# A two-stage front end (modulation, then first norm) made into one stage, with four modulation pieces formed later by GpSimd

## The chip, the cores and the metric

The kernel runs on one core of one Trainium2 chip. The metric is the device time of one execution in microseconds (us), as the median of several runs. A core has a matrix engine (TensorE, PE in the profile, its weight loads PEld), a vector engine (VectorE, DVE), an activation engine (ScalarE, ACT), a general engine (GpSimd, POOL) and an engine that here only starts transfers (SyncE, SP). Engines work through their own instruction streams in order and wait for each other by semaphores. SBUF is the on-chip memory of 128 partitions, PSUM the smaller one that the matrix engine writes.

## The reference

One layer of a diffusion backbone with 2048 latent tokens and 256 context tokens of width 1024. Only the start of it matters here:

```python
sc_lat = jax.nn.silu(c)                 # (1, 1024)
sc_ctx = jax.nn.silu(c_ctx)             # (1024,)
m_lat = split(sc_lat @ w_mod + b_mod, 6)      # w_mod is (1024, 6 * 1024), 24 MB
m_ctx = split(sc_ctx @ w_mod + b_mod, 6)
h_lat = rms_norm(x_lat, norm1_g) * (1 + m_lat[1]) + m_lat[0]
h_ctx = rms_norm(x_ctx, norm1_g) * (1 + m_ctx[1]) + m_ctx[0]
p = h @ w_in                            # the projection, 1024 x 4640
...                                     # two head groups, output projection
x = x + m_lat[2] * y                    # gate; m_lat[3], m_lat[4] modulate the second norm,
                                        # m_lat[5] is the gate of the MLP
```

Pieces 0 and 1 (shift and scale) are needed for the latents and for the context before the projection can start. Pieces 2 to 5 are needed for the latents only, and only in the last stage, after the scans.

## The kernel before

The program is a row of stages (`phase_mod`, `phase_norm`, `phase_project`, `phase_gdn`, `phase_hgrn`, `phase_merge`, `phase_out`). Each stage is a block in which every engine has its own stream. A stage starts on an engine when all engines have ended the one before. Inside a stage the order on each engine is the order in which the code is written, and semaphores tie the engines to each other.

`phase_mod` (L99 to L233). SP loads a few small vectors, then `w_mod` in six pieces of 4 MB into `wm`, two buffers. DVE multiplies each of a piece's eight slices `k` (128 input rows by 1024 columns) by a per-partition number of `sc` and adds it up in `acc` (L214, L217). For pieces 0 and 1 it does so twice, once for the latents and once for the context (`accx`). PE then sums `acc` over the partitions with products of one column (L161, L166), and DVE adds the bias and forms `e.gain` (L227 to L232).

`phase_norm` (L239 to L352). There are five blocks of tokens, one of 256 (context), and four of 512 in a hardware loop. For a block SP loads the tokens (L274), PE transposes them into `pt` (L286), ACT copies them to `xt` (L308) and stores them (L311). DVE squares `xt` slice by slice (L331), PE sums the squares with a matrix of ones (L293), ACT takes the root (L315), DVE the reciprocal of the whole 128x512 result (L333). Then for each slice `k` there are three operations on DVE, the product with the reciprocal (L348), scale and shift (L340) and the remainder `h_lo` (L343), and one on ACT, the rounded half `h_hi` (L319). `h_hi` and `h_lo` are the two halves in which the projection reads its input.

`phase_project` (L364 to L796). For each of 36 tiles of 128 output columns (and a small tile of 32, called ab, at the start), ACT and DVE split the weights into `whi` and `wlo` (L577, L702). PE forms each tile in five groups of tokens (four where the context isn't wanted), each of 24 products into `pg`, with 512 tokens a product (L527). For the first 12 tiles (q, k, v) ACT and DVE do a short convolution and for the first eight a normalisation (L603 to L623, L736 to L751), whose sums run on PE (L541). Tiles are grouped in kinds of four (`KINDS`, L357). GpSimd has nothing to do in these three stages.

```python
331     dve.tensor_tensor(sq[:, k % 2, 0:n], xt[:, k, 0:n], xt[:, k, 0:n], ALU.mult)
333     dve.reciprocal(rt[:, 0:n], rt[:, 0:n])
348     dve.tensor_tensor(ht[:, k % 2, 0:n], xt[:, k, 0:n], rt[:, 0:n], ALU.mult)
455     sp.dma_start(raw[:, 0, :, 0:AB_W], win[:, :, AB_COL:AB_COL + AB_W])
531     pe.wait_ge(w_lo, 1)
```

## Time and profile before

| what | us |
|---|---|
| median of 3 runs | 4352.18 |
| lowest and highest | 4346.83, 4361.99 |
| the profiled execution's own time | 4353.56 |
| its span in the trace | 4351.8 |
| PE busy, share of the span | 83% |
| DVE, ACT, POOL busy | 43%, 32%, 16% |

The profiled execution's time is 1.8 us above its span. The trace holds one execution; times in it are counted from the span's start. A row of the timeline is start, duration, engine, line, operation and operands, and in brackets how long the engine had been idle and what released it. "SPq" and "ACTq" are the issues of transfers. In the views that group instructions, a group's mean duration is in nanoseconds. A product of two plain float32 matrices is two instructions on PE, each with its own weight load; a transpose or a product of the rounded kind (float32r) is one.

### The profile page before, as it was taken

How to read it: one execution, taken by the hardware profiler on the slowest of the kernel's cores; microseconds unless marked ns; L12 is line 12 of the kernel's file. 1: busy time of each engine (PE TensorE's matmuls, PEld its weight loads, DVE VectorE, ACT ScalarE, POOL GpSimd, SP SyncE). 2: the span in 40 equal slices, each digit the busy share in tenths (PEclk: the TensorE clock that was granted, in tenths of full speed). 3: DMA queues.
4: the chain of work that ended last, by engine and by line, in shares of the span. 5: the costliest groups of instructions: out<-in, count | busy, mean ns of one | idle time of the engine just before them, and what ended most of it. 6: DMA issues, size and time to landing. Idle time of an engine off the chain costs nothing. (4 is left out here: it accounts for less than half of the span.)

```text
span 4351.8 us, 98698 instructions
## 1 busy us (share of the span) xinstructions
PE 3614.9 (83%) x42292; PEld 2976.9 (68%) x42292; DVE 1880.8 (43%) x2660; ACT 1377.6 (32%) x1858; POOL 697.0 (16%) x752
## 2 busy tenths in 40 slices
PE   2549999999968888857674428899999888999998
PEld 2327788888857777747664227688888666888886
DVE  7647851111025555545546943523323335233233
ACT  0336641433125555513332212312212223122122
POOL 0000000000035555505556102000000220000002
PEclk9779999999979999966777668899999888999998
DMA  6412232243223333354442263111111231111111
GB/s 234 145 43 49 54 80 75 99 130 100 72 95 109 108 106 113 104 105 85 102 86 70 68 217 107 35 48 52 44 52 46 81 107 35 49 52 44 52 46 58
DMA packets 460370, 365.08 MB, mean 84 GB/s; under 512 B 115908, under 2 KB 413192, under 8 KB 454408
## 3 DMA queue, kind: packets, MB, share of 16 engines
q1 hardware_dynamic: 430088, 315.94, 25.2%
q0 software_dynamic: 6912, 25.17, 1.7%
q10 hardware_dynamic: 23168, 20.97, 1.6%
q8 instruction: 164, 2.69, 0.3%
q14 instruction: 38, 0.31, 0.0%
HBM read 262.64 MB, written 99.39 MB: 83 GB/s over the span
## 5 line engine op out<-in xcount | busy, mean ns | idle before, releaser
L2289 PE MATMUL o_pg<-o_h_hi,o_w_hi 128*128 128x512 f32 x1280 | 516.9, 404 | 70.6 <-DVE o_h_lo L2438 48.6
L527 PE MATMUL p_pg<-h_hi,p_whi 128*128 128x512 f32 (+3 forms) x1384 | 531.4, 384 | 25.5 <-DVE p_wlo L702 25.5
L527 PE MATMUL p_pg<-h_lo,p_whi 128*128 128x512 f32 (+3 forms) x1384 | 519.3, 375 | 0.0
L527 PE MATMUL p_pg<-h_hi,p_wlo 128*128 128x512 f32 (+3 forms) x1384 | 519.3, 375 | 0.0
L2290 PE MATMUL o_pg<-o_h_lo,o_w_hi 128*128 128x512 f32 x1280 | 509.1, 398 | 0.0
L2291 PE MATMUL o_pg<-o_h_hi,o_w_lo 128*128 128x512 f32 x1280 | 509.0, 398 | 0.0
L2289 PE MATMUL o_pg<-o_f_hi,o_w_hi 128*128 128x512 f32 x1024 | 398.3, 389 | 0.0
L2290 PE MATMUL o_pg<-o_f_lo,o_w_hi 128*128 128x512 f32 x1024 | 398.3, 389 | 0.0
L2291 PE MATMUL o_pg<-o_f_hi,o_w_lo 128*128 128x512 f32 x1024 | 398.3, 389 | 0.0
L2289 PEld LDWEIGHTS o_pg<-o_h_hi,o_w_hi 128*128 128x128 f32 x1280 | 245.6, 192 | 150.8 <-issue 46.9
L527 PEld LDWEIGHTS p_pg<-h_hi,p_whi 128*128 128x128 f32 (+1 forms) x1384 | 258.4, 187 | 81.5 <-DVE p_wlo L702 26.3
L2360 ACT ACTIVATE o_w_hi<-o_raw 128x1024 fp32r<-128x1024 f32 x144 | 151.4, 1052 | 484.1 <-PE o_pg L2291 464.7
L2491 DVE SCALAR_TENSOR_TENSOR o_x<-o_pg,mod,o_x 128x512 f32<-128x512 f32 x128 | 96.1, 751 | 469.6 <-PE o_pg L2291 469.6
L527 PEld LDWEIGHTS p_pg<-h_lo,p_whi 128*128 128x128 f32 (+1 forms) x1384 | 258.3, 187 | 55.0 <-issue 6.0
L527 PEld LDWEIGHTS p_pg<-h_hi,p_wlo 128*128 128x128 f32 (+1 forms) x1384 | 258.1, 186 | 50.1
L2291 PEld LDWEIGHTS o_pg<-o_h_hi,o_w_lo 128*128 128x128 f32 x1280 | 247.0, 193 | 52.6
L2290 PEld LDWEIGHTS o_pg<-o_h_lo,o_w_hi 128*128 128x128 f32 x1280 | 247.5, 193 | 48.4
L2482 DVE TENSOR_TENSOR o_tmp<-o_tmp 128x512 f32<-128x512 f32 x128 | 88.6, 692 | 438.1 <-ACT o_f_hi L2409 438.1
L2427 DVE TENSOR_TENSOR o_w_lo<-o_raw,o_w_hi 128x1024 fp32r<-128x1024 f32 x144 | 195.9, 1361 | 71.3 <-ACT o_w_hi L2360 71.3
L2406 ACT ACTIVATE o_tmp<-o_pg 128x512 f32<-128x512 f32 x128 | 76.5, 598 | 470.0 <-PE o_pg L2291 470.0
L2291 PEld LDWEIGHTS o_pg<-o_f_hi,o_w_lo 128*128 128x128 f32 x1024 | 192.3, 188 | 39.9
L2289 PEld LDWEIGHTS o_pg<-o_f_hi,o_w_hi 128*128 128x128 f32 x1024 | 192.3, 188 | 39.9
(279 smaller groups left out, 6265.6 us busy)
## 6 DMA issues: line engine op xcount, KB each, us to landing
o_raw<-in_w_mlp SPq DMA_DIRECT2D x128, 512.0 KB, 4.1
g_kqvb<-scr_kqv SPq DMA_DIRECT2D x72, 384.0 KB, 3.5
mod_w<-in_w_mod SPq DMA_DIRECT2D x6, 4096.0 KB, 13.1
p_raw<-in_w_in SPq DMA_DIRECT2D x38, 512.0 KB, 5.9
g_kqa<-scr_kqv SPq DMA_DIRECT2D x72, 256.0 KB, 3.0
scr_kqv<-p_y SPq DMA_DIRECT2D x24, 576.0 KB, 4.9
scr_hf<-p_y SPq DMA_DIRECT2D x16, 576.0 KB, 5.3
scr_hk<-p_s SPq DMA_DIRECT2D x16, 576.0 KB, 8.2
```

Of the source, the lines that this page charges most:

```text
L527: last = nc.tensor.matmul(pg[0:m, bank, 0:n], w[:, q, k, 0:m], h[:, k, hoff:hoff + n], start=(k == 0 and j == 0), stop=(k == KT - 1 and j ...
L2289: nc.tensor.matmul(out, w_hi[:, p, k, :], half(rhs[0], k, h), start=(k == 0), stop=False)
L2290: nc.tensor.matmul(out, w_hi[:, p, k, :], half(rhs[1], k, h), start=False, stop=False)
L2291: last = nc.tensor.matmul(out, w_lo[:, p, k, :], half(rhs[0], k, h), start=False, stop=(k == KT - 1))
L2360: nc.scalar.activation(w_hi[:, p], raw[:, p], ACT.Copy).then_inc(w_hi_ready, 1)
L2406: nc.scalar.activation(tmp[:, (2 * s + h) % 4, :], pg[:, 2 * (s % 2) + h, :], ACT.Relu).then_inc(rectified, 1)
L2427: dve.tensor_tensor(w_lo[:, p], raw[:, p], w_hi[:, p].bitcast(F32), ALU.subtract).then_inc(w_lo_ready, 1)
L2482: dve.tensor_tensor(slot, slot, slot, ALU.mult).then_inc(f_sq, 1)
L2491: dve.scalar_tensor_tensor(half(x1, m, h), pg[:, 2 * (s % 2) + h, :], e.mod[:, M_GATE2 + m:M_GATE2 + m + 1], half(x1, m, h), ALU.mult, ALU ...
```

## The change

`phase_mod` and `phase_norm` become one stage, `phase_front`. What it does:

- Only pieces 0 and 1 of `w_mod` are loaded there, 8 MB in eight slices of 1 MB (rows `k`, 2048 columns), into four buffers that lie in the space of `h_lo`. PE multiplies each slice with the two columns of `sc` (latents, context) as the stationary side, 4 products of 512 columns a slice (`products`), and adds up in PSUM. ACT and DVE copy the two rows out (`mrow`), PE turns them into columns with 16 transposes, DVE adds the bias and forms the gain.
- Tokens are loaded in tiles of 128 rows. ACT (three tiles of a block, and both of the context) and DVE (one tile) square each row and add it up in the same instruction (`square`). The root and the reciprocal are taken of 128x4 numbers. DVE puts them on a diagonal (`diag`), and PE spreads them over all partitions with four products with the ones (`spread`).
- Per slice `k`, ACT copies the transposed tokens (`copy`) and forms `h_hi` (`high`). DVE forms product, gain and norm in one operation (`scale`) and the remainder in another (`low`). The squares of the next block stand among the slices of the present one.
- The 14 small loads move from SP to ACT. The tokens' transpose is stored by SP in two halves a block. The first two weight loads of the projection are issued in the front stage.
- `h_hi` and `h_lo` are five tensors each, one for each block.
- In `phase_project` GpSimd forms pieces 2 to 5 in eight sums `c` of 512 columns. For each of a sum's eight slices it loads 256 KB from its own queue, multiplies by `sc` and adds to `macc`. After every fourth tile PE sums `macc` over the partitions (`mod_sums`, 4 products of one column) into unused columns of bank 0 of `pg`. At the end of the stage DVE adds the bias and forms the second gain.

The core of the diff:

```diff
+                for k in range(4):
+                    load_w(k)
+                load_x(0)
+                for k in range(4, KT):
+                    load_w(k)
+                load_x(1)
+                load_x(2)
...
+                store(1)
+                load_x(3)
+                store(2)
+                load_x(4)
+                store(3)
+                store(4)
...
+                def products(k):
+                    pe.wait_ge(wm_in[k % 4], 16 * (k // 4 + 1))
+                    for n in range(4):
+                        last = nc.tensor.matmul(mp[0:2, n, :], e.sc[:, k, :], wm[k % 4][:, n, :],
+                                                start=(k == 0), stop=(k == KT - 1))
...
+                def spread(b):
+                    pe.wait_ge(diag_ready, b + 1)
+                    if b >= 2:
+                        pe.wait_ge(u_ready, 8 * (b - 1))
+                    for a in range(BLOCKS[b][0]):
+                        last = nc.tensor.matmul(mp[:, b % 2, a * P:(a + 1) * P], e.ones, diag[:, a, :], start=True, stop=True)
...
+                for b in range(1 + NB):
+                    for k in range(KT + 1):
+                        if k < KT:
+                            copy(b, k)
+                        if k >= 1:
+                            high(b, k - 1)
+                        if 1 <= b < NB and 3 <= k < 6:
+                            square(b + 1, k - 3)
+                        if 1 <= b < NB and k == 6:
+                            roots(b + 1)
...
+                    dve.scalar_tensor_tensor(ur[:, g % UR, 0:n], xt[:, g % RING, 0:n], e.gain[:, g0 + k:g0 + k + 1],
+                                             mp[:, b % 2, 0:n], ALU.mult, ALU.mult).then_inc(u_ready, 1)
...
+                    dve.scalar_tensor_tensor(e.h_lo[b][:, k, :], ur[:, g % UR, 0:n], e.mod[:, s0 + k:s0 + k + 1],
+                                             e.h_hi[b][:, k, :].bitcast(F32), ALU.add, ALU.subtract).then_inc(lo_ready, 1)
...
+                def mod_sums(c, released):
+                    pe.wait_ge(m_acc, c + 1)
+                    pe.wait_ge(group_free, released)
+                    for s in range(TB // P):
+                        last = nc.tensor.matmul(modps[:, c * 4 + s:c * 4 + s + 1], macc[:, s * P:(s + 1) * P],
+                                                e.ones[:, 0:1], start=True, stop=True)
...
+                    pool.wait_ge(mw_in[x % 2], 16 * (x // 2 + 1))
...
+                        nc.gpsimd.tensor_scalar(w, w, sc, None, ALU.mult).then_inc(m_part, 1)
+                        pool.wait_ge(m_part, done + 1)
+                        nc.gpsimd.tensor_tensor(macc[:, :], macc[:, :], w, ALU.add).then_inc(m_part, 1)
+                        done += 2
...
+                    if x + 2 < MC * KT:
+                        load(x + 2)
```

How the instructions stand, first on DVE at the end of the modulation (before), where `mod_acc` is the running sum of a piece:

```order
L214 TENSOR_SCALAR mod_acc<-mod_w,mod_sc 128x1024
L217 SCALAR_TENSOR_TENSOR mod_acc<-mod_w,mod_sc,mod_acc 128x1024 x7
L227 TENSOR_TENSOR mod<-mod_ps,cols 128x48
L228 TENSOR_TENSOR mod<-mod_ps,cols 128x16
L232 SCALAR_TENSOR_TENSOR gain<-mod,cols 128x8 x3
```

and on PE in the changed front stage, where `n_wm_50` to `n_wm_53` are the four buffers of `w_mod`, `n_pt` the transposed tokens, `n_mrow` the two modulation rows and `n_diag` the diagonals:

```order
L211 MATMUL n_mp<-n_wm_52,sc 2x512 x4
L211 MATMUL n_mp<-n_wm_53,sc 2x512 x4
L222 MATMUL n_pt<-cst,n_x 128x128 x6
L248 MATMUL n_cc<-cst,n_mrow 128x2 x16
L231 MATMUL n_mp<-n_diag,cst 128x128 x2
L222 MATMUL n_pt<-cst,n_x 128x128 x10
L222 MATMUL n_pt<-cst,n_xb 128x128 x4
L231 MATMUL n_mp<-n_diag,cst 128x128 x4
L222 MATMUL n_pt<-cst,n_xb 128x128 x28
```

The weighted sum over the input rows has moved from DVE to PE, which does it 4 products at a time as the slices come in. One block's first transposes stand ahead of the `spread` for it, the other 28 behind it.

DVE in a block of 512 tokens, before (from the squares to the second slice):

```order
L331 TENSOR_TENSOR n_sq<-n_xt 128x512
L332 REGISTER_ALU
L333 RECIPROCAL n_rt<-n_rt 128x512
L348 TENSOR_TENSOR n_ht<-n_xt,n_rt 128x512 x2
L340 TENSOR_SCALAR n_ht<-n_ht,gain,mod 128x512
L343 ISA
L343 TENSOR_TENSOR h_lo<-n_ht,h_hi 128x512
L348 TENSOR_TENSOR n_ht<-n_xt,n_rt 128x512
```

and now (the end of one block and the start of the next; `n_u` is what `scale` writes):

```order
L394 SCALAR_TENSOR_TENSOR n_u<-n_xt,gain,n_mp 128x512
L402 SCALAR_TENSOR_TENSOR h_lo<-n_u,mod,h_hi 128x512
L375 RECIPROCAL n_rs<-n_rs 128x4
L380 TENSOR_SCALAR n_diag<-cst,n_rs 128x128 x4
L402 SCALAR_TENSOR_TENSOR h_lo<-n_u,mod,h_hi 128x512
L394 SCALAR_TENSOR_TENSOR n_u<-n_xt,gain,n_mp 128x512 x2
```

Three operations for a slice are two, the eight squares are one instruction elsewhere in the block, and the reciprocal is of 4 columns in place of 512, followed by four products for the diagonal.

PE in the projection, at the end of the fourth tile (now; `p_macc` is GpSimd's sum):

```order
L608 MATMUL p_pg<-h_hi,p_wlo 128x512
L622 MATMUL p_pn<-p_s,cst 128x512
L628 MATMUL p_pg<-cst,p_macc 128x1 x4
L608 MATMUL p_pg<-h_hi,p_whi 128x256
L608 MATMUL p_pg<-h_lo,p_whi 128x256
```

The row of four one-column products is new, and stands at eight such places; before, a tile's last product was followed at once by the next tile's first.

## Rows read from the trace of the kernel before

**Rows 1.** Busy time of each engine by stage (granted clock, share of the DMA engines, GB/s)

```profile
0.00:109.00 109.00, 28.91 (x130) 28.11 (x130) 78.70 (x80) 3.05 (x5) 0.21 (x4) 1.00 0.61 234
109.00:263.00 154.00, 66.72 (x224) 41.56 (x224) 108.52 (x166) 55.15 (x87) 0.00 (x0) 0.72 0.34 120
263.00:340.00 77.00, 51.84 (x226) 34.16 (x227) 26.00 (x20) 27.11 (x31) 0.00 (x0) 0.79 0.11 25
340.00:590.00 250.00, 235.94 (x1057) 184.97 (x1056) 204.46 (x167) 164.04 (x214) 0.00 (x0) 1.00 0.26 59
590.00:1222.00 632.00, 631.00 (x2952) 529.31 (x2951) 87.99 (x100) 193.31 (x228) 0.00 (x0) 1.00 0.32 93
```

**Rows 2.** Timeline, from the start to the first norm's first block

```profile
0.75 1.28 ACT L174 ACT_TABLE_LOAD   x1 [0.75 <-PEq L2552]
...
1.20 0.42 SPq L135 DMA_DIRECT2D mod_rows<-in_b_mod  x1
...
6.98 74.30 SPq L149 DMA_DIRECT2D mod_w<-in_w_mod  x6
...
104.34 3.57 PE L161 MATMUL mod_ps<-cst,mod_acc 128*128 128x1 f32 x16 [8.81 <-DVE mod_acc L217]
...
113.75 3.63 PE L286 MATMUL n_pt<-cst,n_x 128*128 128x128 f32 x16 [5.84 <-DMA n_x<-in_ctx]
```

**Rows 3.** Timeline, roots of two blocks running, then the norm's end and the projection's start

```profile
207.13 0.69 ACT L315 ACTIVATE n_rt<-n_pq,eps 128x512 f32<-128x512 f32 x1 [7.06 <-PE n_pq L293]
...
237.86 0.69 ACT L315 ACTIVATE n_rt<-n_pq,eps 128x512 f32<-128x512 f32 x1 [7.06 <-PE n_pq L293]
...
257.84 0.69 DVE L343 TENSOR_TENSOR h_lo<-n_ht,h_hi 128x512 f32 x1 [0.15 <-DVE n_ht L340]
...
263.34 0.42 PE L527 MATMUL p_pg<-h_hi,p_whi 128*32 128x256 f32 x1 [25.52 <-DVE p_wlo L702]
```

**Rows 4.** Timeline of PE, the last four float32 instructions of 512 columns in a block

```profile
143.56 1.99 PE L293 MATMUL n_pq<-n_sq,cst 128*128 128x512 f32 x4
```

**Rows 5.** Groups of ACT between 108 and 264 us (busy, mean ns | idle before)

```profile
L319 ACT ACTIVATE h_hi<-n_ht,mod,gain 128x512 f32 x32 | 25.6, 812 | 47.7 <-DVE n_ht L348 47.7
L308 ACT ACTIVATE n_xt<-n_pt 128x512 f32<-128x512 f32 x32 | 17.3, 595 | 2.0 <-PE n_pt L286 1.2
L319 ACT ACTIVATE h_hi<-n_ht,mod,gain 128x256 fp32r<-128x256 f32 x8 | 4.7, 598 | 6.4 <-DVE n_ht L348 6.4
L308 ACT ACTIVATE n_xt<-n_pt 128x256 f32<-128x256 f32 x8 | 3.1, 384 | 104.0 <-PE n_pt L286 103.8
L577 ACT ACTIVATE p_whi<-p_raw 128x1024 fp32r<-128x1024 f32 x1 | 1.1, 1057 | 1.1 <-DMA p_raw<-in_w_in 1.1
```

**Rows 6.** Groups of DVE in the projection: from PSUM, and with two SBUF inputs

```profile
L702 DVE TENSOR_TENSOR p_wlo<-p_raw,p_whi 128x1024 fp32r<-128x1024 f32 x37 | 45.2, 1223 | 245.1 <-ACT p_whi L577 241.3 <-DVE p_s L786 2.9 <-DVE p_s L792 1.0
L741 DVE SCALAR_TENSOR_TENSOR p_y<-p_pg,cols,p_y 128x512 f32<-128x512 f32 x36 | 27.0, 751 | 63.4 <-ACT p_y L603 62.8
L751 DVE TENSOR_TENSOR p_y<-p_y,p_rt 128x512 f32<-128x512 f32 x32 | 22.1, 692 | 1.1
```

**Rows 7.** DMA issues (KB each, median us from issue to landing)

```profile
n_x<-in_ctx SPq DMA_DIRECT2D x1, 1024.0 KB, 4.9
scr_ga<-p_y SPq DMA_DIRECT2D x4, 1024.0 KB, 4.7
```

**Rows 8.** Groups of POOL in the whole span

```profile
L2253 POOL TENSOR_TENSOR o_rt<-o_rt,o_tmp 128x512 f32<-128x512 f32 x56 | 71.7, 1289 | 148.2 <-ACT o_tmp L2367 148.0
L2269 POOL DMA_DIRECT2D o_ring<-scr_xT x16 | 8.8, 548 | 110.4 <-DVE o_x L2447 99.4 <-DVE o_h_lo L2438 11.0
L2250 POOL COPY o_rt<-o_tmp 128x512 f32<-128x512 f32 x8 | 4.8, 615 | 1292.3 <-ACT o_tmp L2367 1292.2
```

**Rows 9.** A DVE group beside a busy POOL, 1226 to 1890 us: two SBUF inputs

```profile
L1342 DVE TENSOR_TENSOR g_z<-g_z,g_vt 128x512 f32<-128x512 f32 x36 | 38.0, 1055 | 0.0
```

**Rows 10.** PE's waits between 340 and 590 us (total us, times, longest)

```profile
PE p_pn L541 <- ACT p_s L614: 14.1, 15, 1.8
```

More of the change, by code:

```diff
@@ new lines, in high @@
+                def high(b, k):
+                    g = 8 * b + k
+                    nt, g0, s0 = BLOCKS[b]
+                    act.wait_ge(u_ready, g + 1)
+                    nc.scalar.activation(e.h_hi[b][:, k, :], ur[:, g % UR, 0:nt * P], ACT.Identity,
+                                         bias=e.mod[:, s0 + k:s0 + k + 1]).then_inc(hi_ready, 1)
+                for a in range(2):
+                    square(0, a)
+                roots(0)
+                for a in range(3):
+                    square(1, a)
@@ new lines, in _ @@
+                roots(1)
+                act.wait_ge(wm_used, KT)
+                nc.scalar.activation(mrow[:, 0:2, :], mp[0:2, 0:2, :], ACT.Copy).then_inc(mrow_act, 1)
+                for b in range(1 + NB):
[8 more added lines that the diff above has]
+                            roots(b + 1)
@@ new lines, in _ @@
+                last.then_inc(mod_ready, 1)
+                dve.wait_ge(mod_ready, 1)
+                for b in range(1 + NB):
+                    for k in range(KT + 1):
+                        if k < KT:
+                            scale(b, k)
+                        if k >= 1:
+                            low(b, k - 1)
+                        if b == 0 and k == 2:
+                            inverse(1)
+                        if 1 <= b < NB and k == 4:
+                            square(b + 1)
+                        if 1 <= b < NB and k == 7:
+                            inverse(b + 1)
```

441 lines of the change are left out of this document (244 added, 197 removed).

## The prediction

> **What bounds the kernel now.** First the busy times by stage [rows 1]. The reader should see two kinds of stage. Up to 263 us PE is busy for 28.9 of 109 and 66.7 of 154 us, and DVE for 78.7 and 108.5: nothing of the projection runs, and everything waits for a chain that goes through DVE. From 590 us on PE is busy for 631 of 632 us; between, from 340, for 235.9 of 250. So a microsecond taken out of the first 263 is a microsecond of the end, and one added to PE after 340 is one too. Second, the timeline of the start [rows 2]: the six loads of `w_mod` are issued until 81 us, the last sums of PE end at 107.9, and the first tokens are transposed at 113.8, because their load is only issued after the stage has ended. Third, the norm [rows 3]: two roots of neighbouring blocks are 30.7 us apart (237.86 - 207.13), the last `h_lo` ends at 258.5, and the first product of the projection starts at 263.3, after a load and a split of its weights. The front end is thus 263.3 us long, 108 of modulation, 6 of waiting for tokens, 145 of norm, 5 to get going.
>
> **The new front stage, step by step.** I add it up to the projection's first product.
>
> 1. Products begin. They need the first slice and the two silu columns. The first slice is SP's fourth issue, at about 2.2 us, and 1 MB lands 4.9 us after its issue [rows 7]: 7.1. ACT first issues 14 small loads; on SP 16 issues took 6.98 - 1.20 = 5.8 us, 0.36 each [rows 2], so 5.1 from 0.75 on, then a table load of 1.28 and the silu: 7.4. Both come together; I take 7.4.
> 2. 32 products of 512 float32 columns, two instructions each. Four such instructions took 1.99 us with the drain of the last [rows 4], so 0.50 at most and 0.46 by my estimate without the drain: 32 x 0.92 = 29.5. The first slice will run at the lower clock, at twice that: +3.7. The loads are not behind: 8 MB and the context's 1 MB, against 234 GB/s as the mean of a stage that was held up by DVE [rows 1], would be 40 us at that rate, and 1 MB in 4.9 us with its latency is already about the pace of 3.7 us a slice with four buffers. End of products: 40.6.
> 3. Two copies out of PSUM of 1024 columns, side by side on ACT and DVE, 2 x 0.6 = 1.2 (0.595 for 512 [rows 5]). 16 transposes: 16 instructions of this size took 3.57 and 3.63 us [rows 2]: 3.6. Bias and gain 0.7. Together 5.5: 46.1. Squares, roots and the first diagonals are done by then, beside the products.
> 4. Context block, paced by ACT: 8 x (0.384 + 0.598) = 7.9 [rows 5]: 54.0.
> 5. A block of 512. ACT: 8 x (0.595 + 0.812) = 11.3, three squares of 1024 columns at 1.06 (the nearest row of that size) = 3.2, root 0.2: 14.7 [rows 5]. DVE: 8 x (0.75 + 0.70) = 11.6 [rows 6], the fourth square 1.3, reciprocal and four diagonals 1.0: 13.9. They run side by side, so 14.7. At the border they don't: the diagonals are made late in DVE's order, PE then needs 8 instructions at 0.22 [rows 2] = 1.8 to spread them, and the first `scale` 0.75 before ACT has a `high`: 2.6. A block is 17.3 in place of 30.7. Three of them: 51.9, and the last, without squares, 11.3 + 0.7. End at 117.9.
> 6. The stage also waits for its last store. It is issued when the last slice is copied, some 2.3 us before the end, and 1 MB takes 4.7 to land [rows 7]: +2.4, 120.3.
> 7. The projection's first weights are there already, so only the two splits of 32 columns and the start of a stage remain: 1.4, where it was 4.8. First product at about **122 us**, 141 earlier.
>
> **Bounds of that.** At best ACT never waits at the borders (-8) and the transposes go at the higher clock (-2): 112. At worst all products run at the lower clock: below.
>
> **What the projection pays.** PE's one-column products move into a stage where PE is full. They are 8 x 4, two instructions each, 64 in all. In the modulation 16 took 3.57 us [rows 2], 0.22 each, 14.3 as the upper bound; the lower is none of it where PE waits anyway. It waits 14.1 us between 340 and 590 [rows 10], where three of the eight places are; five are where it doesn't wait at all. I take 10, since at the higher clock they should be quicker than in that row: range 5 to 14. Waiting for GpSimd is not to be feared: a slice costs it a multiplication, an addition and an issue. Addition 1.29, issue 0.55 [rows 8]; the multiplication isn't in the trace, and lies between the copy, 0.62, and the addition, 1.29. That is 2.5 to 3.1, and with a wait for the load at most 4, so 32 us for a sum; a kind takes PE four tiles, some 90 us (1222 - 340 over 35 tiles is 25 each). The order on GpSimd has nothing else queued. DVE pays at its side: operations with two SBUF inputs take 0.69 for 512 columns in the projection [rows 6], and 1.06 where GpSimd is busy beside it [rows 9], 0.36 more. GpSimd will be busy for a third of each kind. In the q and k kinds DVE is busy for 204 of 250 us [rows 1] and PE's sums hang on it; some 13 such operations meet GpSimd there, 4.7 us on DVE, of which I put 2 on PE (0 to 5). After 590 DVE is idle for most of the time and hides it. The bias and gain at the stage's end are DVE's, while PE still works on its last tile; the 16.8 MB of loads lie where the DMA engines are a quarter to a third busy [rows 1].
>
> The Trainium skill (SBUF — State Buffer, "SBUF: two separate sides") says that DVE and GpSimd share a pair of SBUF ports as an exclusive lock held for a whole instruction, so that a DVE operation with two SBUF inputs is blocked until a GpSimd one ends. The 1.06 against 0.69 agrees in kind, though it is less than a whole GpSimd addition of 1.29; by the rule at its hardest each meeting would cost 1.29 in place of 0.36, so 17 us on DVE in q and k instead of 4.7, and the sum would be worse by up to 12 us. The same page warns that loads issued by GpSimd can be starved by DVE; no row here shows that.
>
> **The sum.** The profiled execution took 4353.6 us: -141 + 10 + 2 = -129, so 4224.6. The median of the runs lies 1.4 below the profiled one: **4223 us**.
>
> **Rivals.**
>
> - *The clock stays low in the products.* They have a stationary side of only two columns, and the trace has no such instruction. For it: in the first 109 us the profile records 1.00, yet 16 instructions took the same 3.6 us as in the stage that was granted 0.72 [rows 1, 2], so the low level, 1.2 GHz, is what such thin work got. Against it: PE has no gaps here. Price: 59 us in place of 33.2, 26 more: 4249. Chance 0.12.
> - *The blocks wait for tokens.* The load of block 3 is issued after block 1 has been copied, behind 1 MB of store. 3 MB then land within some 11 us, and ACT wants the third tile about 10 us into the block. A slower store costs up to 4 us a block, three times: 4235. Chance 0.09.
> - *The projection pays more.* All 37 + 32 operations with two SBUF inputs [rows 6] slowed by 0.36, and PE waiting for each, is 25 us; with 14 of sums: 4250. Against it: after 590 nothing of DVE is urgent. Chance 0.10.
> - *The front is shorter still* (borders hidden, products at the pace of the loads): 4200. Chance 0.06.
> - *Slower than before: PE waits for GpSimd.* `mod_sums` stands in PE's order, and all later tiles are queued behind it. From 263 to the last place, about 1135, there are 872 us for 64 slices. Above 13.6 us a slice PE begins to wait, and above 13.6 + 129/64 = 15.6 the change is slower than before: at 16 it would be 4380. The rows give at most 4, so this needs a load that takes over four times its normal time. Chance 0.03.
>
> **The numbers.** The forecast has 0.60, with 4207 to 4240 as its own range. The range for 8 in 10 takes in the slow tokens, the clock and most of a costlier projection: 4204 to 4258. A measurement of this kernel can tell about 0.3%, 13 us, from no change. All cases but the last are far beyond that: faster 0.96, same 0.01, slower 0.03 (the last case, from a slice of 15.4 us on).
>
> **What would show it.** The first product of the projection at 112 to 130 us; the 32 products in 30 to 36 us at a granted clock of 1.00 (if near 60, the clock rival); neighbouring roots 16 to 19 us apart; before the first `scale`, no wait of PE or ACT for tokens; from there to the projection's end 5 to 20 us more than the 959 of before, with one-column products of 0.1 to 0.22 us each; no wait of PE for `p_macc`; DVE's two-input operations longer in the first third of each kind. After the projection all stages should be as long as before; if one isn't, the sum is wrong in a place that I haven't looked at.

## The result and the profile after

The changed kernel takes 4208.24 us (median of 4 runs, 4195.76 to 4209.89), against 4355.73 us for the kernel before on the same chip (4 runs, 4346.83 to 4361.99). The ratio is 0.9657, 95% interval 0.963 to 0.9683: 3.4% faster. Forecast was 4223 with a range of 4204 to 4258.

| stage | before, us | changed, us | difference | forecast |
|---|---|---|---|---|
| up to the projection's first product | 263.34 | 111.44 | -151.9 | -141 |
| projection, to GpSimd's first MEMSET behind it | 962.95 | 971.05 | +8.1 | +12 |
| all behind | 3125.5 | 3125.3 | -0.2 | 0 |
| span | 4351.8 | 4207.8 | -144.0 | -129 |

The changed kernel by stretch of time, as [rows 1] for before. A row is the stretch, its length, each engine's busy time with its instructions, the granted clock, the share of the DMA engines and GB/s:

```profile
core 0: us, PE busy (x) PEld busy (x) DVE busy (x) ACT busy (x) POOL busy (x), PEclk, DMA share, GB/s
0.00:7.95 7.95, 0.28 (x1) 0.18 (x1) 0.09 (x2) 1.50 (x3) 0.21 (x4) 1.00 0.70 251
7.95:38.40 30.45, 30.45 (x66) 5.67 (x66) 3.33 (x14) 9.17 (x16) 0.00 (x0) 1.00 0.83 322
38.40:41.80 3.40, 2.81 (x31) 2.58 (x30) 1.71 (x5) 1.54 (x3) 0.00 (x0) 1.00 0.02 5
41.80:49.75 7.95, 5.39 (x25) 4.12 (x23) 7.53 (x21) 6.06 (x15) 0.00 (x0) 0.62 0.44 136
49.75:97.80 48.05, 23.23 (x122) 20.00 (x121) 39.50 (x71) 37.01 (x69) 0.00 (x0) 0.68 0.71 254
97.80:111.44 13.64, 3.80 (x26) 2.85 (x24) 10.86 (x17) 9.93 (x17) 0.41 (x1) 0.75 0.40 154
111.44:1082.49 971.05, 927.17 (x4296) 756.77 (x4296) 329.61 (x288) 383.31 (x472) 223.60 (x184) 0.98 0.37 96
1082.49:4207.80 3125.31, 2614.25 (x37706) 2167.75 (x37706) 1376.08 (x2128) 934.80 (x1294) 696.41 (x748) 0.89 0.26 78
```

Read the second row first: PE is busy for all of its 30.45 us, where before the modulation was DVE's and took 109 us [rows 1]. The norm's context block, three full blocks and the last one took 145 us before; they now lie in rows four to six and take 67 us (41.8 to 109.05). The same stretches in the timeline (start, duration, engine, line, operands, number; in brackets the idle time ahead and what ended it), which answer to [rows 2] and [rows 3]:

```profile
6.42 1.28 ACT L279 ACT_TABLE_LOAD   x1 [6.42 <-issue]
7.71 0.18 ACT L279 ACTIVATE sc<-n_cc 128x16 f32<-128x16 f32 x1
7.95 2.72 PE L211 MATMUL n_mp<-n_wm,sc 128*2 128x512 f32 x3 [3.69 <-ACT sc L279]
...
17.68 20.76 PE L211 MATMUL n_mp<-n_wm,sc 128*2 128x512 f32 x48
...
39.84 1.12 PE L248 MATMUL n_cc<-cst,n_mrow 2*128 2x2 f32 x16 [0.59 <-DVE n_mrow L408]
...
59.87 0.29 ACT L300 ACTIVATE n_rs<-n_ss,eps 128x4 f32<-128x4 f32 x1
63.18 2.08 PE L231 MATMUL n_mp<-n_diag,cst 128*128 128x128 f32 x8 [4.86 <-DVE n_diag L380]
65.35 0.75 DVE L394 SCALAR_TENSOR_TENSOR n_u<-n_xt,gain,n_mp 128x512 f32<-128x512 f32 x1 [1.56 <-issue]
66.15 0.60 ACT L310 ACTIVATE n_xt<-n_pt 128x512 f32<-128x512 f32 x1 [3.44 <-PE n_pt L222]
75.90 0.29 ACT L300 ACTIVATE n_rs<-n_ss,eps 128x4 f32<-128x4 f32 x1
```

The last 48 product instructions took 20.76 us, 0.43 each. The first ones were slower: three took 2.72 us, with starts 0.85 us apart, twice the 0.43, and the first sixteen took 9.54 us:

```profile
7.95 9.54 PE L211 MATMUL n_mp<-n_wm,sc 128*2 128x512 f32 x16 [3.69 <-ACT sc L279]
```

At 0.43 us each sixteen would take about 7.0, so some six of them ran at the lower level of the clock, 1.2 GHz, behind an idle time of PE of 3.69 us. The table's 1.00 doesn't contradict that: in this trace the records of the granted clock begin at 13.04 us, and a stretch without a record is printed as 1.00.

Two roots are 16.0 us apart (75.90 - 59.87), 30.7 before. At the border between two blocks PE stands 4.86 us for the diagonals and ACT 3.44 us for the transposes queued behind them; e7 returns to that.

In the projection, the two kinds of GpSimd arithmetic and the one-column sums of PE (engine, operation, number: shortest, median, longest in ns, first and last start):

```profile
L669 POOL DMA_DIRECT2D p_mw<-in_w_mod x64: 557/590/1562, 111.0 to 916.7; - x64
L685 POOL TENSOR_SCALAR p_mw<-p_mw,sc x56: 1558/1572/2400, 117.2 to 922.8; 128x512 f32<-128x512 f32 x56
L687 POOL TENSOR_TENSOR p_macc<-p_macc,p_mw x56: 1270/1290/2302, 118.9 to 924.5; 128x512 f32<-128x512 f32 x56
...
  PE p_pg L628: 547.9, 7
```

GpSimd waited for PE for 547.9 us in seven waits (78 us each), and PE never for GpSimd. The whole list of PE's waits in the projection is these two rows (waiting line, released by: us in total, times, longest); the second is the projection's start:

```profile
PE p_pn L622 <- ACT p_s L738: 38.5, 15, 25.0
PE p_pg L608 <- DVE p_wlo L826: 8.6, 1, 8.6
```

### The profile page after: what moved, and what is told of

It is laid out like the page before. It is cut to its first block and busy times, and to the rows that moved or that the text cites. A ratio compares the mean times of both kernels' runs of the same rounds, so it can differ in the third digit from the quotient of the medians.

```text
span 4207.8 us, 98568 instructions
## 1 busy us (share of the span) xinstructions
PE 3607.4 (86%) x42264; PEld 2959.9 (70%) x42264; DVE 1768.7 (42%) x2544; ACT 1383.3 (33%) x1887; POOL 920.6 (22%) x936
```

## The experiments

Eleven variants and a repetition of the changed kernel ran. A single total can't settle a few microseconds here: the stages behind the projection, which no variant touches, took between 3112.7 us (e1) and 3125.5 us (before). The totals were also measured on several chips, on which the median of the kernel before lay between 4352.5 and 4357.4. So the variants are compared by two stretches of their traces, the start of the projection and its length, and where these differ by 3 us or less, by the rows in which they differ. The start itself moves by 1.3 us between kernels with the same front (110.15 to 111.44), mostly because three to seven of the first product instructions run at the lower clock, a different number in each execution. The third column leaves that out: it counts from the end of the products to the projection's first product, and is 72.87 to 73.00 us in all six profiles with an unaltered front.

| kernel | projection starts | from the products' end | its length | total, us (runs) |
|---|---|---|---|---|
| before | 263.34 | - | 962.95 | 4355.73 (4) |
| changed | 111.44 | 73.00 | 971.05 | 4208.24 (4) |
| changed, again | 110.15 | 72.89 | 968.72 | 4201.56 (5) |
| e1, deferral alone | 219.93 | - | 970.03 | 4303.59 (4) |
| e2, four times the sums | 111.27 | 72.98 | 1005.09 | 4236.06 (1) |
| e3, GpSimd only loads | 110.27 | 72.87 | 967.53 | 4201.61 (1) |
| e4, slow GpSimd | 110.46 | 72.87 | 1215.61 | 4447.68 (1) |
| e5, wide reciprocals | 124.27 | 85.75 | 971.26 | 4214.23 (1) |
| e6, tokens behind the modulation | 124.65 | 87.28 | 971.94 | 4215.64 (1) |
| e7, early inverse | 105.26 | 67.41 | 973.61 | 4208.53 (4) |
| e8, GpSimd late | 111.42 | 72.99 | 969.94 | 4207.02 (1) |
| e9, e7 and e8 | 104.85 | 67.11 | 972.56 | 4194.44 (5) |
| e10, DVE's low half twice | 125.07 | 86.91 | 968.85 | 4212.58 (1) |
| e11, ACT's high half twice | 125.90 | 87.23 | 969.20 | 4214.83 (1) |

### e1: the deferral alone

The edit is to the kernel before: two pieces in the modulation stage, and the changed kernel's GpSimd block and shifted sums in the projection.

```diff
-        PIECES = 6
+        PIECES = 2
...
+                def mod_sums(c, released):
...
+            @block.gpsimd
+            def _(pool):
```

> The kernel before with one part of the change alone: the modulation makes two of its six pieces ahead of the projection, and GpSimd forms the other four while the projection runs, with the sums over partitions between the projection's tiles. The first modulation stage and the first norm stay two stages in the old form. My theory: the four pieces left out were about 12 us each of the stage that waits for the loads and for GpSimd, so the time ahead of the projection falls by about 50 us (263 to about 213 us), the projection grows by 8 us as in the changed kernel (eight places of 1.0 us), the later stages stay: total about -42 us, near 4312. The rival: most of the gain is the deferral, since the modulation stage is bound by the eighteen pieces of work on six pieces, and the stage falls to a third (109 us to about 37): time ahead of the projection -73 us, total -65, near 4289. A third: the projection pays more without the merged front, because DVE and GpSimd compete as they did there: projection +20 or more.

Measured: ratio to before 0.9887 (0.9871 to 0.9904), -49 us. By stage (the old norm is the second row):

```profile
0.00:65.30 65.30, 14.62 (x66) 14.16 (x66) 39.36 (x45) 3.05 (x5) 0.21 (x4) 1.00 0.34 133
65.30:219.93 154.63, 66.78 (x225) 41.49 (x225) 108.97 (x168) 55.21 (x87) 1.25 (x2) 0.73 0.34 119
219.93:1189.96 970.03, 926.32 (x4296) 756.03 (x4296) 327.61 (x288) 383.89 (x472) 225.54 (x182) 0.98 0.37 96
```

The start of the projection moves by 43.4 us, not by 50 or 73: each piece left out gives 43.4 / 4 = 10.9 us. The old stage goes on at 65.3 where it went on at 109; the norm is unchanged (154.6, before 154.3). The projection pays 7.1 us. So the first theory (213 us and a projection 8 us longer) is nearer than its two rivals, a start 73 us earlier and a projection 20 us longer. The deferral alone is worth 36 us by the stages that it touches, a quarter of the change's 144; the other 13 us of its total lie in stages that it doesn't touch. The larger part of the change is the merged stage: 219.93 - 111.44 = 108.5 us, of which the modulation by PE's products is 65.3 - 41.8 = 23.5 and the norm the remaining 85.

### e5, e6: two parts of the norm undone

```diff
-                    dve.reciprocal(rs[:, t:t + n], rs[:, t:t + n]).then_inc(inv, 1)
...
                         dve.wait_ge(bc_ready, b + 1)
+                        dve.reciprocal(mp[:, b % 2, 0:n], mp[:, b % 2, 0:n]).then_inc(inv, 1)
```

> The changed kernel with one part of the new norm undone: the reciprocal of the root is taken of the row spread over 128x512 (3.35 us each, 1.75 us for the context's 256 columns, as in the kernel before) in place of the 128x4 column ahead of the spreading. My theory, that a block's period of 16.0 us ends on VectorE around the border between blocks, since ScalarE is busy for 12.35 us of it: the reciprocal stands after the spreading and ahead of the block's first product, so each of the blocks pays its 3.35 us in full, 4 x 3.35 + 1.75 = 15 us later start of the projection (111.4 to about 126.5). The rival, that ScalarE's copies and roundings bound the block: the reciprocal lies beside them and the start moves by under 5 us.

Measured: the projection starts 12.8 us later. The reciprocals by themselves (first of a block, then the next):

```profile
70.01 3.37 DVE L388 RECIPROCAL n_mp<-n_mp 128x512 f32<-128x512 f32 x1 [1.57 <-PE n_mp L231]
88.69 3.37 DVE L388 RECIPROCAL n_mp<-n_mp 128x512 f32<-128x512 f32 x1 [1.58 <-PE n_mp L231]
```

The period is 18.68 us against 16.02: 2.66 of the 3.37 are paid; the rest is hidden, presumably beside what the other two engines had left to do meanwhile. The first theory holds, somewhat weaker than its 15 us.

In e6 the loads of the tokens go behind the modulation, and the first block's squares with them:

```diff
-                for k in range(4):
+                for k in range(KT):
                     load_w(k)
+                sp.wait_ge(mod_ready, 1)
                 load_x(0)
-                for k in range(4, KT):
-                    load_w(k)
                 load_x(1)
```

> The changed kernel with another part undone: the tokens' loads wait until the modulation is done, as they did in the kernel before, and the squares and sums of the first block move behind them into the context block. The theory of the merged stage: ahead of the context block stand now a load's landing (4.9 us), the transposes, copies and squares of it (3 to 5 us) and the first root and reciprocal (about 3 us), and the context block itself gets the first token block's squares on top: the start of the projection moves from 111.4 to about 124 us (12 to 14 us later). The rival: what stands ahead of the blocks is hidden under the 30 us of the modulation's products anyway, so little of the 152 us gained comes from the overlap: under 5 us later.

Measured: 13.2 us later, 14.3 counted from the end of the products, as the first theory had it:

```profile
40.21 0.25 DVE L408 SCALAR_TENSOR_TENSOR gain<-mod,cols 128x8 f32<-128x8 f32 x2
44.16 1.06 ACT L291 ACTIVATE n_junk<-n_x 128x1024 f32<-128x1024 f32 x1 [5.74 <-DMA n_x<-in_ctx]
...
46.58 1.28 ACT L299 ACT_TABLE_LOAD   x1
47.87 0.29 ACT L299 ACTIVATE n_rs<-n_ss,eps 128x2 f32<-128x2 f32 x1
...
50.35 0.87 DVE L388 SCALAR_TENSOR_TENSOR n_u<-n_xt,gain,n_mp 128x256 f32<-128x256 f32 x2 [1.40 <-PE n_mp L230]
```

Gain and bias are there at 40.5, and the first scaling comes at 50.35 in place of 41.82: load, squares, table, root, diagonals and spreading stand in a row, 8.5 us. The other 4.7 lie behind it, where the context block now has the token squares of the first block as well. e5 and e6 account for 27 of the norm's 85 us, if their costs may be added. The rest, 58 us, wasn't undone piece by piece, so its cause is argued and not shown: three DVE operations on a slice became two, and the squares left DVE and PE, three tiles of four for ACT. What the traces show is DVE's busy time between modulation and projection, 108.8 us before, 57.9 now (7.53 + 39.50 + 10.86), and the same in one period from root to root, before and now:

```profile
207.13:237.86 30.73, 14.49 (x48) 8.80 (x48) 23.44 (x33) 11.30 (x17) 0.00 (x0) 0.72 0.36 139
59.87:75.90 16.03, 7.46 (x40) 6.51 (x40) 13.04 (x24) 12.34 (x25) 0.00 (x0) 0.71 0.71 262
```

Of the 14.7 us that a period lost, DVE's busy time lost 10.4 and its idle time 4.3.

### e10, e11: which engine paces a block

```diff
+                    if b < NB:
+                        dve.scalar_tensor_tensor(e.h_lo[NB][:, k, 0:n], ...)
```

e10 repeats DVE's second operation of a slice, e11 in the same way the rounding on ACT.

> The changed kernel with VectorE's second operation on every slice of the norm (the low half) issued twice in all blocks but the last, the extra one into memory that the last block overwrites; same result. It adds 8 x 0.66 = 5.3 us of VectorE's time to each block of 512 tokens; VectorE is busy for 13.0 and ScalarE for 12.3 of a block's 16.0 us. Theory A, the prediction's: ScalarE's 14.7 us pace a block and VectorE's work lies beside it with some 3 us to spare, so the period grows by 5.3 - 3.0 = 2.3 us, to about 18.3. Theory B: VectorE sets the pace, since the chain at the border between two blocks (reciprocal, diagonals, first product) is its own, so it pays all of it: period 21.3 us, start of the projection 3 x 5.3 + 2.6 = 18 us later (about 129 us in place of 111.4; by theory A about 119).

> The counterpart: ScalarE's rounding to the high half issued twice on every slice in all blocks but the last; same result. It adds 8 x 0.5 to 0.6 = 4 to 4.9 us of ScalarE's time to a block. Theory A, ScalarE paces a block: it pays all of it, period 20 to 20.9 us, start of the projection about 3 x 4.5 + 2 = 15 us later (near 127 us). Theory B, VectorE sets the pace and ScalarE has 16.0 - 12.3 = 3.7 us to spare: the period grows by about 1 us, to 17.2, and the start by 4 us, to 115. Should both kernels pay in full, a block is one chain that goes through both engines, and neither paces it alone.

Measured: period 19.77 us with DVE's operation doubled (roots at 63.64 and 83.40) and 20.15 us with ACT's (65.54 and 85.69). ACT pays nearly in full: added activations start 0.61 us apart though each lasts 0.72, so eight of them are 4.9 us, of which the period pays 4.13. DVE pays 3.74 of 5.3 us. The projection starts 13.9 us later with DVE's work doubled, between theory A's 7.6 and theory B's 17.6, and 14.2 us later with ACT's, as theory A said (15). So theory A is right on ACT and too generous on DVE, which has 1.6 us to spare in a block, not the 3.0 of its idle time. Neither engine paces a block alone: work added to either is mostly paid, ACT's a little more than DVE's. In e11 DVE waits 5.2 us for ACT's copies, and ACT for nothing ahead of the added operation (groups, busy, mean ns | idle before and what ended it, 65 to 105 us):

```profile
L397 DVE SCALAR_TENSOR_TENSOR n_u<-n_xt,gain,n_mp 128x512 f32<-128x512 f32 x17 | 12.7, 746 | 8.3 <-ACT n_xt L310 5.2 <-issue 3.1
L317 ACT ACTIVATE h_lo<-n_u,mod 128x512 fp32r<-128x512 f32 x17 | 12.3, 723 | 0.0
```

### e2, e3, e8: what the projection pays for

e2 makes each place's four one-column products sixteen; e3 leaves pieces 2 to 5 of the modulation out of the computation (GpSimd loads the weights but only fills its sum with a constant); e8 computes all, but behind the projection's first twelve tiles, with a place after every second tile there.

```diff
-                    for s in range(TB // P):
+                    for s in [t % 4 for t in range(4 * TB // P)]:
```

> The changed kernel with the four one-column products in each of the eight places between the tiles made sixteen (each column written four times, same result). It tells apart what makes the projection of the changed kernel 8.1 us longer than before (971.05 against 962.95 us). Theory A, the shifted sums themselves: 1.0 us per place of four products, so twelve more cost 3.0 us a place and the projection grows by about 24 us, to about 995 (up to 37 us if each added product costs its two weight loads of 192 ns in full). Theory B, contention of DVE with GpSimd: TensorE waits for DVE's longer operations, and the added products change little, under 5 us.

```diff
-                        nc.gpsimd.tensor_scalar(macc[:, :], w, sc, None, ALU.mult).then_inc(m_part, 1)
+                        nc.gpsimd.memset(macc[:, :], 0.5).then_inc(m_part, 1)
...
-                        nc.gpsimd.tensor_scalar(w, w, sc, None, ALU.mult).then_inc(m_part, 1)
-                        pool.wait_ge(m_part, done + 1)
-                        nc.gpsimd.tensor_tensor(macc[:, :], macc[:, :], w, ALU.add).then_inc(m_part, 1)
```

> The changed kernel in which GpSimd issues the same 64 loads of the modulation's weights during the projection but does no arithmetic on them (one memset per sum in place of fifteen operations): pieces 2 to 5 of the modulation are left out of the computation, with constants in their place. Theory A, the shifted sums cost the 8.1 us: the projection stays at 971 us (within 1.5), though DVE's two-input operations fall back to the durations of the kernel before (1311 to about 1223 ns, 741 to about 692 ns) if GpSimd's arithmetic is what lengthens them. Theory B, contention costs the 8.1 us: the projection falls to about 963 to 965 us. If the DVE durations stay long, the loads and not the arithmetic lengthen them.

e2 measured +34.0 us: between theory A's 24 and its upper 37, and not theory B. The place itself, in the changed kernel and in e2:

```profile
286.04 0.95 PE L628 MATMUL p_pg<-cst,p_macc 128*128 128x1 f32 x8
286.85 0.36 PE L608 MATMUL p_pg<-h_hi,p_whi 128*128 128x256 f32 x1
```

```profile
285.79 3.63 PE L628 MATMUL p_pg<-cst,p_macc 128*128 128x1 f32 x32
289.28 0.56 PE L608 MATMUL p_pg<-h_hi,p_whi 128*128 128x256 f32 x1
```

A place costs PE 0.81 us (286.85 - 286.04) and 3.49 us with sixteen products, so 2.68 more, 21.4 for eight places. The other 12.6 us came by another way. The first place of e2 and the window behind it:

```profile
285.83:289.28 3.45, 3.45 (x33) 3.45 (x32) 3.38 (x5) 2.45 (x3) 0.00 (x0) 1.00 0.00 0
289.28:292.63 3.35, 3.35 (x17) 3.35 (x17) 3.31 (x3) 3.00 (x5) 2.68 (x3) 0.50 0.00 0
```

PE is busy throughout, and yet the granted clock of the second row is 0.50, 1.2 GHz: 3.35 us at half speed lose about 1.7. In front of it stood 3.49 us of nothing but one-column products. The clock fell so during or behind seven of the eight places of e2, for 3.4 us at three and 6.8 us at four, 37.5 us in all, but not behind the third, where sixteen products of the same 3.49 us were followed by 6.83 us granted 1.00:

```profile
519.79:523.28 3.49, 3.49 (x33) 3.49 (x32) 2.16 (x3) 1.59 (x3) 0.00 (x0) 1.00 0.01 2
523.28:530.11 6.83, 6.83 (x32) 5.68 (x32) 1.23 (x1) 2.02 (x3) 5.67 (x5) 1.00 0.72 136
```

The distance from the third place to the fourth is 2.68 us more than in the changed kernel, just the products. Behind the other places it is 4.2 to 5.9 us more, but for the first (0.4), behind which the changed kernel's first profile lost time too. So the 12.6 us are the clock's; what spares the third place stays open. In the changed kernel the clock fell at none of the eight. The sums scale worse than linearly; four at a place are cheap, and sixteen mostly cost the clock as well.

e3 measured 967.53 us, 3.5 less than the changed kernel's first profile, and DVE's operations fell back as expected: 1309 to 1222 ns for the 128x1024 subtraction and 741 to 692 for the 128x512 product, within 1 ns of [rows 6]. Neither theory had 967.5. The first profile of the changed kernel has one thing that e3's hasn't (DVE, then GpSimd, then PE):

```profile
307.64 1.55 DVE L875 TENSOR_TENSOR p_y<-p_y,p_rt 128x256 f32<-128x256 f32 x1
```

```profile
307.62 1.29 POOL L687 TENSOR_TENSOR p_macc<-p_macc,p_mw 128x512 f32<-128x512 f32 x1
```

```profile
312.02 1.12 PE L622 MATMUL p_pn<-p_s,cst 128*128 128x512 f32 x2 [2.40 <-ACT p_s L738]
...
313.45 0.63 PE L608 MATMUL p_pg<-h_hi,p_wlo 128*128 128x512 f32 x1
```

One two-input operation of DVE takes 1.55 us beside GpSimd's arithmetic (0.43 in e3), ACT gets its input later, PE stands 2.40 us, and then runs products of 0.63 in place of 0.39 us for some 3 us: granted clock 0.50 from 313.4 to 316.8. The Trainium skill (SBUF — State Buffer, "SBUF: two separate sides") has a DVE operation with two SBUF inputs and a GpSimd operation that reads SBUF exclude each other for a whole instruction. This meeting agrees: GpSimd's addition began 0.02 us ahead, and the DVE operation ended 0.28 us behind its end, +1.12 us. The mean of the 32 operations of 512 columns rose by only 49 ns. Whether the two meet here differs from one execution to the next: in the repetition of the changed kernel this operation took 0.43 us, and PE's wait was 1.30 us in place of 2.40.

To see whether that meeting costs every execution something, e8 moves GpSimd's work to where PE never waits:

```diff
+                pool.wait_ge(w_lo, QKV + 1)
                 load(0)
                 load(1)
```

> The changed kernel with GpSimd's whole work on the modulation moved behind the projection's first twelve tiles (q, k and v, where TensorE waits now and then for ScalarE and VectorE), into the last six kinds, with the shifted sums after every second tile there (every tile pair, eight places, as many products as before). Theory, from the removal of GpSimd's arithmetic: it costs 2.5 to 6 us of the projection through VectorE's longer operations and a TensorE clock that falls behind a longer wait (one such fall at 312 us of the changed kernel), all of it in the first twelve tiles, because in the later ones TensorE is busy 30.00 of 30 us; so the projection falls from 971 to about 966 to 968 us. The eight places of products still cost about 0.6 us each. The rival: the later tiles wait for VectorE's longer operations too, or TensorE waits for the sums, which now have 44 us each in place of 100: then 971 or more.

> The changed kernel once more, unaltered, on the chip of the two runs before it, as their comparison. It also shows how far one execution differs from another in the two parts that are compared: the start of the projection (111.4 us in the first profile) and its length (971.05 us); both should come within 1 us and 2 us of these, the total between 4196 and 4212.

e8's projection took 969.94 us, and the unaltered changed kernel, run again, 968.72, with no fall of the clock behind the wait at 309 (312 in the first profile). So moving GpSimd gained nothing that can be told, and the theory that its arithmetic costs 2.5 to 6 us falls: e3 is 1.2 us below the repetition, and two profiles of the changed kernel differ by 2.3. What remains of the 8.1 us is the eight places, 8 x 0.81 = 6.5 us, less what lies in PE's waits, plus, in the first profile (and in e7's), a clock that fell behind one of these waits. In e8, where no place lies near a wait, the projection is 7.0 us longer than before's; in the repetition, where two of the eight do, it is 5.8.

### e4: GpSimd too slow

```diff
+                        for _ in range(9):
+                            nc.gpsimd.tensor_scalar(w, w, 1.0, None, ALU.mult).then_inc(m_part, 1)
```

> The changed kernel with GpSimd's work on a slice of the modulation's weights made longer: nine more multiplications by one, of 1.56 us each, on seven of every eight slices, so that a sum takes about 3.3 + 7 x 18.2 = 131 us in place of 34. It tests the prediction's slower rival, that TensorE waits for GpSimd once a sum takes longer than a kind of the projection (about 100 us between two places of the shifted sums). Theory: TensorE's queue stands at each of the eight places until the sum is there; since a sum begins only when the one before it was read, the eighth place moves from 990 us to about 286 + 7 x 131 = 1203 us if the first place is met in time, and the total grows by about 210 us, to about 4420: slower than the kernel before. The rival: the wait is hidden because TensorE has a tile in hand; then the total stays within 20 us of 4208. DVE's operations beside the longer GpSimd work should also stay long throughout.

Measured: 4447.68 us, 95 over the kernel before on the same chip (4352.54), and 28 over the 4420 expected. The waits of PE:

```profile
PE p_pg L628 <- POOLq L695: 220.7, 7, 46.8
PE p_pn L622 <- ACT p_s L742: 40.9, 16, 25.8
```

The projection is 244.6 us longer than the changed kernel's first, 24 more than these waits. The clock stood at 0.50 for a while behind each of them:

```profile
549.51:557.36 7.85, 7.85 (x23) 6.50 (x24) 0.00 (x0) 0.00 (x0) 5.86 (x6) 0.50 0.23 67
```

The 5.0 to 7.9 us at half speed behind the seven waits add up to some 23 us lost, so here a wait of PE costs more than its length. A place of four products that falls into such a stretch takes 1.73 us in place of 0.81.

The places now lie (1230.5 - 285.7) / 7 = 135 us apart, the time of one sum, against 100.6 before, and PE stands in seven of the eight. The slower rival is real, and its size right: by the prediction's threshold of 13.6 us a slice, 135 / 8 = 16.9 gives 4224 + 64 x 3.3 = 4435. The kernel has 3.7 to 4.6 us a slice (29.4 to 36.7 a sum).

### e7, e9: two attempts at a better order

```diff
-                        if 1 <= b < NB and k == 6:
+                        if 1 <= b < NB and k == 5:
                             roots(b + 1)
...
-                        if 1 <= b < NB and k == 7:
+                        if 1 <= b < NB and k == 5:
                             inverse(b + 1)
```

> The changed kernel with the order of two small steps moved: the roots of the next block are taken by ScalarE one place earlier (after the fifth square) and their reciprocals by VectorE two places earlier. Theory: the border between two blocks is a chain of root, reciprocal, spreading over the partitions and first product, 2.1 + 1.6 + 3.4 us of waits at 63 to 69 us of the profile; with the reciprocal ready before the border, about 1.5 us of each of the three borders goes, the period falls from 16.0 to about 14.6 us and the projection starts 4 to 6 us earlier (at about 106 to 107 us), total near 4203. The rival: the border is set by ScalarE's copies and the spreading itself, which still come after the last square, and the period stays at 16.0: no change. Should the earlier steps make ScalarE or VectorE stand for a square or a sum not yet there, the period grows by up to 1 us.

> The two orders together: roots and reciprocals of the next block earlier, and GpSimd's work behind the first twelve tiles. Theory: the two gains add, since one is ahead of the projection and one in it: start of the projection at 105.3 us, projection 966 to 968 us, so 9 to 10 us under the changed kernel, near 4199. The rival: what the projection gives back (it took 973.6 us behind the earlier start) eats the first gain: within 3 us of the changed kernel.

e7's roots are 13.96 and 14.64 us apart, and the projection starts at 105.26, 4.9 us before the repetition of the changed kernel and 6.2 before its first profile, 5.5 us earlier counted from the end of the products: the border's chain was exposed, as said. But its projection is the longest apart from e2's and e4's, 973.61. The clock around the projection's second wait, one window of the changed kernel:

```profile
196.44:201.44 5.00, 3.81 (x15) 2.82 (x16) 4.93 (x4) 4.76 (x7) 0.00 (x0) 1.00 0.00 0
```

Two windows of e7 at the same place, and the wait in its timeline of PE:

```profile
190.26:195.26 5.00, 3.22 (x10) 1.79 (x9) 4.93 (x5) 3.80 (x6) 0.00 (x0) 0.75 0.00 0
195.26:200.26 5.00, 5.00 (x22) 4.07 (x21) 4.93 (x6) 4.11 (x6) 0.00 (x0) 0.91 0.00 0
```

```profile
192.59 1.91 PE L622 MATMUL p_pn<-p_s,cst 128*128 128x512 f32 x2 [1.78 <-ACT p_s L738]
```

The wait is 1.78 us in both kernels (at 197.63 in the changed one), but in e7, e9 and e6 the clock fell behind it and in the other profiles it held. What decides that stays open: the work around the wait is the same in all. By total e7 is 4208.53 us, ratio 0.9658 (0.9642 to 0.9674), no different from the changed kernel; e9 has 0.9629 (0.9608 to 0.9651) against 0.9645 (0.9627 to 0.9663) for the repetition on the same chip. The 7 us between their medians are within what the runs scatter, so no faster kernel is shown. e9's first theory (966 to 968 us for the projection) fell with e8's.

## The prediction, point by point

**The bottleneck** was read rightly: a microsecond out of the first 263 was one off the end, and all behind the projection stayed as it was.

**1, start of the products**: 7.4 forecast, 7.95 measured; ACT's table load began at 6.42 rather than 5.85 (0.75 + 5.1), its fourteen issues taking longer than SP's.

**2, the 32 products**: 33.2 forecast, 30.45 measured. The price per instruction was 0.43 us where 0.46 was taken, 1.9 us in all. The lower clock at the start came as forecast, though for six instructions and not eight: 2.5 us in place of 3.7, by the starts 0.85 us apart up to 13.03 us. The 1.00 in the table isn't evidence against it, since nothing is recorded before 13.04; the prediction had seen the same contradiction in the modulation of before. The rival of a clock that stays low, 4249, fell with the other 58 instructions at 0.43; with two stationary columns PE too was granted 2.4 GHz, from 13.04 us on.

**3, copies and transposes**: 5.5 forecast, 3.4 measured (38.4 to 41.8). The mis-sized term is the sixteen transposes: 1.12 us, not 3.6. They were priced by the one-column products of [rows 2], 0.22 us each. That is the price at the lower clock: a place of eight such instructions takes 0.81 us at 1.00 (0.10 each) and 1.73 at 0.50 (0.22 each, e4). At the higher clock sixteen would be 1.6, which the prediction's bound (-2) allowed for. The last 0.5 us may be the kind or the shape of the instruction (the products' weights have 128 partitions, these have two); no run tests it.

**4, context block**: 7.9 forecast, 7.95 measured.

**5, blocks**: 17.3 forecast, 15.6, 16.0 and 16.0 measured from first scaling to first scaling (49.75, 65.35, 81.38, 97.40); the last 12.0 against 11.65. The sum of ACT's durations, 14.7, counted eight `high` at 0.812, which took 0.717. Beyond that, neighbours on ACT overlap: an activation that lasts 0.72 us is followed by the next one 0.61 after its start, and durations added up overstate a row of them. ACT is busy for 12.3 us of the 16.0, where 14.7 were taken, and it stands 3.7 us, where 2.6 were allowed, 3.44 of them at the border. Two errors of opposite sign, so the 16.0 is nearer to the forecast than its parts are.

**6 and 7, store and start**: 4.1 us forecast between the last `low` and the first product (117.9 to 122), 2.4 measured (109.05 to 111.44). The front's end is thus 10.6 us earlier than forecast: 2.2 from the first two steps together, 2.1 from the third, 4.6 from the blocks, 1.7 from here.

**The projection**: 10 us for the sums and 2 for DVE, against 5.8 to 8.1. A place was taken at 1.25 us and measured 0.81; the range of 5 to 14 held. Of the eight places two lie where PE waits, not three as the prediction had it: the last such wait of the changed kernel is at 386 us, and the third place at 514.6. DVE's lengthening was right in kind (+87 ns on the subtraction, +49 on the product, +1.12 us on the 256-column product at 307.64). Its price was taken at 2; e3 against the repetition gives 1.2, which is less than the 2.3 by which the kernel's own two profiles differ, so it may be nothing. The price of GpSimd's multiplication was wrong: it was bounded by 0.62 and 1.29 and took 1.56. A slice is then 1.56 + 1.29 + 0.59 and the gaps between them, 3.9 us; a sum took 29.4 to 36.7 us, 31.9 on average, so the text's 4 for a slice held in the mean by its allowance for a load. The wrong price cost nothing, since the threshold was 13.6. The Trainium skill (GPSIMD Engine Reference, "Engine selection") calls one-input work on GpSimd roughly line-rate; here a one-input multiplication took longer than the two-input addition.

**Rivals.** Slow tokens, 4235: the period is the same 16.03 and 16.02 us for the two inner blocks, and no wait of ACT or DVE in them is for a load. A costlier projection, 4250: the reason against it held; from 441 to 1071 us PE is busy for 630.00 of 630 us. The shorter front, 4200, had a chance of 0.06. The front was shorter by 10.6 us, but by neither of its two reasons: the borders stayed, and the products ran at PE's pace (busy for all of 30.45 us), not at that of the loads. The sum of the parts, 4224.6 - 10.6 - 3.9 = 4210.1, is within 0.5 us of the profiled 4209.57. The forecast was right for its reasons, and 15 us too long because five of its terms (products, transposes, blocks, the start of the projection, what the projection pays) were taken too high, and none too low by more than 0.6. The errors nearly all had one sign, and the result lies at the low end of the range: the repetition's median on another chip, 4201.56, is below it.

## What to carry to other kernels

Work that nobody needs yet is best put where its engine idles and read out at points that the busy engine passes anyway; the price is the read-out (0.8 us a place here), and the condition is that a part is ready within the distance of two places. Once a sum waits for it, all queued behind waits too, and here a tenth more, because the clock fell in the waits (244.6 us for 220.7 of them). When two engines hand a slice back and forth, add up the distances between starts and not the durations, and look at the border between blocks for a short chain through three engines: there 2.7 us of a 3.4 us operation were paid. And where a trace's clock reads 1.00, check that it was recorded at all: instructions of one kind that are twice as long as the same ones later say more.

## What was not expected of the hardware

- The granted clock fell to 0.50 at seven of eight places with 3.49 us of one-column products, with PE busy throughout, and at none of the eight with 0.81 us of them.
- The first six product instructions ran at half speed (starts 0.85 us apart, then 0.43), behind 3.69 us without work on PE, while the profile printed a clock of 1.00 for want of a record.
- Eight one-column instructions took 0.81 us at a granted clock of 1.00 and 1.73 at 0.50 (e4).
- The clock fell behind the same wait of 1.78 us in three profiles and not in the others.
- A one-input operation of DVE lengthened beside GpSimd's arithmetic too: a `TENSOR_SCALAR` on 128x2304 took 1822 ns in the mean of eight, up to 2431, against 1414 in e3 and 1415 before.
- GpSimd's multiplication of 128x512 by a scalar column took 1.56 us, its addition of two such tiles 1.29 and its copy 0.62 [rows 8].
- The stages behind the projection, the same instructions in all kernels, took 3112.7 to 3125.5 us, 0.4%. No edit touches them, and two profiles of the unaltered changed kernel alone differ by 4.8 us there.
